# Recurrent mixer of the even layer without the products over constants that TensorE does while VectorE and ScalarE form weights

## What is computed

```python
def step(carry, inp):
    C, n, m = carry
    qc, kc, vc, ic, fc = inp
    b = jnp.cumsum(fc, axis=-1)
    log_d = jnp.where(tril, b[..., :, None] - b[..., None, :] + ic[..., None, :], -jnp.inf)
    log_inter = m[..., None] + b
    m_t = jnp.maximum(log_inter, jnp.max(log_d, axis=-1))
    w_intra = jnp.exp(log_d - m_t[..., None]) * jnp.einsum('bhtd,bhsd->bhts', qc, kc)
    ...
    num = (w_inter[..., None] * jnp.einsum('bhed,bhtd->bhte', C, qc)
           + jnp.einsum('bhts,bhse->bhte', w_intra, vc))
    ...
    C = decay[..., None, None] * C + jnp.einsum('bhs,bhse,bhsd->bhed', w_s, vc, kc)
```

## Time and profile before

| what | us |
|---|---|
| median of 3 runs | 3340.39 |
| the profiled execution's own time | 3338.58 |
| its span in the trace | 3336.8 |
| TensorE matmuls busy in the span | 3025.6 (91%) |
| mLSTM steps 2 to 5 (about 1997 to 2086 us of the span) | 89 |

### The profile page before, as it was taken

How to read it: one execution, slowest core, us unless ns; L and a number is a source line. 1 busy time by engine, 2 the same in 40 slices (tenths; PEclk the granted TensorE clock), 3 DMA queues, 4 the chain that set the end, 5 groups by cost and what they waited for, 6 DMA issues and landing times.

```text
span 3336.8 us, 41503 instructions
## 1 busy us (share of the span) xinstructions
PE 3025.6 (91%) x18502; PEld 2036.5 (61%) x18502; DVE 1112.0 (33%) x1572; ACT 877.3 (26%) x1320; POOL 0.2 (0%) x4
## 2 busy tenths in 40 slices
PE   6997899999997899999899988889999976999998
PEld 3775778888765777888677667554433353443443
DVE  3446632242536543223343347420000136000002
ACT  3443232232544233223433531311000032010001
POOL 0000000000000000000000000000000000000000
PEclk9998999999998899999899999889999997999999
DMA  7224323223233222222552041379999932999996
GB/s 267 78 99 152 103 76 98 92 95 95 79 116 148 68 89 89 92 92 95 177 163 74 13 192 62 106 294 409 409 408 409 401 133 101 364 409 409 408 409 268
DMA packets 247442, 637.27 MB, mean 191 GB/s; under 512 B 12896, under 2 KB 110176, under 8 KB 247136
## 3 DMA queue, kind: packets, MB, share of 16 engines
q1 hardware_dynamic: 244128, 627.22, 50.6%
q10 hardware_dynamic: 3136, 7.40, 0.6%
HBM read 632.48 MB, written 2.10 MB: 190 GB/s over the span
## 4 chain that ended last, share of the span: by engine, by line
PE 72%; DVE 8%; DMA 6%; ACT 5%; PEld 4%; issue 3%; PEldq 1%; SPq 1%; ACTq 0%; DVEq 0%
PE ps L612 69%; PEld ps L612 4%; DMA ring<-in_w_exp_gate 3%; PE ps L626 3%; ACT h L1580 1%; PEldq L1083 1%; DMA proj<-in_w_exp_gate 1%; ACT mix_halves L1583 1%; DMA ring<-in_w_exp_up 1%; DMA ring<-in_ada_w 1%; SPq L600 1%; ACT proj L1997 0%; DMA ring<-in_w_mod 0%; DVE work L2288 0%; DVE work L2881 0%
## 5 line engine op out<-in xcount | busy, mean ns | idle before, releaser
L612 PE MATMUL ps<-mix_halves,work_halves 128*128 128x512 f32 (+1 forms) x1544 | 622.1, 403 | 44.4 <-DVE h_halves L2139 34.4
L612 PE MATMUL ps<-h_halves,work_halves 128*128 128x512 f32 (+1 forms) x1544 | 608.9, 394 | 4.8 <-ACTq L1494 2.4
L612 PE MATMUL ps<-mix_halves,ring_halves 128*128 128x512 f32 x1448 | 568.3, 392 | 0.0
L2139 DVE TENSOR_TENSOR ring_halves<-ring,work_halves 128x2048 fp32r<-128x2048 f32 (+2 forms) x125 | 252.6, 2021 | 550.4 <-ACT work_halves L1503 453.9
L612 PE MATMUL ps<-ring,work 128*64 128x512 f32 x1680 | 389.1, 594 | 20.9 <-DMA ring<-in_w_exp_gate 18.2
L612 PEld LDWEIGHTS ps<-mix_halves,work_halves 128*128 128x128 f32 (+1 forms) x1544 | 290.8, 188 | 130.9 <-issue 48.8
L612 PEld LDWEIGHTS ps<-h_halves,work_halves 128*128 128x128 f32 (+1 forms) x1544 | 291.7, 189 | 72.6 <-issue 6.4
L612 PEld LDWEIGHTS ps<-mix_halves,ring_halves 128*128 128x128 f32 x1448 | 272.6, 188 | 60.8
L612 PEld LDWEIGHTS ps<-ring,work 128*64 128x64 f32 x1680 | 128.0, 137 | 254.6 <-issue 254.3
L2539 DVE SCALAR_TENSOR_TENSOR x<-ps,small,x 128x512 f32<-128x512 f32 x112 | 82.3, 750 | 598.5 <-PE ps L612 597.0
L1503 ACT ACTIVATE work_halves<-ring 128x2048 fp32r<-128x2048 f32 x102 | 188.2, 1845 | 337.2 <-PE ps L612 336.1
(11 more groups left out here) (377 smaller groups left out, 3318.1 us busy)
## 6 DMA issues: line engine op xcount, KB each, us to landing
ring<-in_w_exp_gate SPq DMA_DIRECT2D x114, 1024.0 KB, 11.3
ring<-in_w_exp_down SPq DMA_DIRECT2D x100, 1024.0 KB, 13.0
ring<-in_w_exp_up SPq DMA_DIRECT2D x96, 1024.0 KB, 15.2
ring<-in_ada_w SPq DMA_DIRECT2D x48, 1024.0 KB, 7.1
ring<-in_w_mod SPq DMA_DIRECT2D x48, 1024.0 KB, 7.5
proj<-in_w_exp_up SPq DMA_DIRECT2D x28, 1024.0 KB, 12.8
proj<-in_w_exp_down SPq DMA_DIRECT2D x28, 1024.0 KB, 15.9
ring<-in_w_in SPq DMA_DIRECT2D x22, 1024.0 KB, 5.3
```

The source lines that it names most:

```text
L612: i = pe.matmul(o, lhsT, rhs, start=start, stop=stop, **kw)
L2139: to("lo", tt(rounded(v), v, rounded(hi), ALU.subtract))
```

## The change

The helper `keep_busy` and its one call are taken out. In each of the steps 2 to 5 TensorE goes from the products of item 2 straight to the wait for `m_w`. Nothing else differs, except that lines behind the edit have numbers lower by 5 or 6.

```diff
             def mlstm():
 
-                def keep_busy(bank, times):
-
-                    for _ in range(times):
-                        mm(ps[:, bank, :], ident, consts[:, 0:T], True, True)
-
                 def vector(i, bank):
...
                         if step == 2:
                             mod_turn(4, 5)
                             pe.wait_ge(*due("mod_ready"))
-                        keep_busy(4, 6)
                         pe.wait_ge(*due("m_w"))
```

## The result

The changed kernel takes 3350.43 us (median of 7 runs, 3346.29 to 3355.72) against 3337.19 us (7 runs, 3329.89 to 3344.84) for the kernel before (the 3340.39 us ahead of the prediction is the median of the first three of these seven). The ratio is 1.0038, with a 95% interval of 1.0023 to 1.0054: slower by 0.38%, about 13 us. The forecast was 3352 us, with a range of 3343.5 to 3358.5; it was built on the profiled execution of before, 3338.58 us, and the profiled one of the changed kernel took 3351.80.

A forecast was written before the change was run, and what follows sets the result against it. VectorE and ScalarE bound each step's first part, TensorE the second. With the clock lost, 3 x 4.3 + 2.25 - 1.6 = 13.6 us on top of 3338.58 us gives 3352 us, range 3343.5 to 3358.5.

The forecast's parts named there:

- the first part of the prediction: In steps 2 to 5 VectorE and ScalarE set the first part, TensorE the second, some 8 us, where the price falls.
- The gain: Step 2: transposes start right behind line 2746 and end at 2010.42 instead of 2012.04, 1.6 us; steps 3 to 5 nothing.
- The cost: Second parts of steps 2 to 5 begin at 1.2 GHz: 4.3 us each in steps 2 to 4, 2.25 in step 5.
- transposes: Start of each step's second part: 8 transposes take 1.84 us at the low clock against 1.09, 0.75 us more.
- one-column products at the low clock: Behind the transposes: paced by their weight loads, 3.39 us against 1.86, 1.5 us more; lower bound nothing.
- values: The m_num products in each step's second part: 3.52 us at the low clock against 2.03, 1.5 us more.
- update, until the clock returns: Behind the values in steps 2 to 4: 1.1 us runs slowly, clock back 4.6 us after the values start; costs 0.55 us.
- step 5, both ends of the path: No update, values already slow: both ends move by what transposes and one-column products lose, 2.25 us.
- starts of steps 3, 4, 5: From the spreading to VectorE's pick-up: no difference, with bounds of 1.7 us less or 1.1 us more.
- The early return: Rival, steps 2 to 5: clock returns some 4.1 us after the first transpose; 6.0 us more, 3344.6 us; chance 0.16.
- That the clock outlasts the gap: Rival: clock stays high over gaps of 6.4 and 6.6 us; only the 1.6 us gain remains, 3337.0 us; chance 0.07.
- that it doesn't return before a step's end: Rival: update and last one-column products slow too, 6.9 us a step; 22.4 us more in all, 3361 us; chance 0.07.

The follow-up runs named there:

- the step 2 run: The kernel before with the six products over constants left out in step 2 alone, kept in steps 3 to 5: 3339.46 us, ratio 1.0013.
- the run with three and seven products: The kernel before with three products over constants in step 2 and seven in steps 3 to 5, instead of six: 3337.73 us, ratio 0.9995.

## Why the prediction was right

**The bound and the place.** All of the difference is in steps 2 to 5, and within them in the part that TensorE sets, as the first part of the prediction had it. VectorE's chain ahead of m_w keeps its length: from the start of line 2714 to the end of line 2740 it is 10.1 us in step 3 after (2025.36 to 2035.45), and 10.1 us from line 2720 to the end of line 2746 before.

**The gain.** Predicted 1.6 us in step 2. The first transpose stands 12.2 us into the stage (2009.14) instead of 13.8 (2011.01 in the timeline before), 1.6 us earlier. Three products in step 2 show the same with the clock held.

**The cost.** The table holds the terms of the sum against what they measured in steps 2, 3 and 4, as differences from one group's start to the next.

| term | predicted, us | measured, us |
|---|---|---|
| transposes | 0.75 | 0.8 to 0.9 |
| one-column products at the low clock | 1.5 | 1.6 |
| values | 1.5 | 1.5 to 1.7 |
| update, until the clock returns | 0.55 | 0, 0.2 and 0.5 |
| step 5, both ends of the path | 2.25 | 2.4 |
| starts of steps 3, 4, 5 | 0 | -0.9, -0.7, +1.3 |

The one-column products, for which no row stood at 1.2 GHz, took 3.41 us in every step: the upper end, and so the choice that they are paced by their weight loads, was right. With 64 columns they took 3.51 us, hardly more, which bears it out. The return of the clock came 3.1 to 4.6 us behind the start of the values, mostly sooner than the 4.6 us assumed, so the update's term was the one that was too large, by some 0.3 us a step. The values were priced a little too low: the 3.52 us that the prediction took as wholly slow ended at 2086.23, and the clock was back at 2085.8; wholly slow they took 3.73 to 3.76 us. By steps the stage grew 2.3, 3.4, 3.9 and 3.7 us, in all 13.2 us; the prediction's sum was 13.6.

Some of this closeness is luck. The starts of steps 3 to 5 add up to only -0.3 us because they cancel: step 5's alone cost 1.3 us, more than the 1.05 us that the prediction had for a slow start. In the second trace of the changed kernel they add up to -1.5 us, and its stage was 101.0 us. The second parts are where the sum was right: from the first transpose to VectorE's start on the last product they grew by 3.9, 4.3 and 4.6 us in steps 2 to 4, against the 4.3 of the forecast.

The slow stretches of the second parts are 8.1, 9.0 and 9.6 us in steps 2 to 4, together 26.7 us, and cost 12.8 us. (The 8.6 us of step 5 can't be added, since its values ran slowly before already.) The rule of the Trainium skill ("TensorE: Matmul & The Clock Gate", on the clock gate's oscillation) that a throttled stretch costs half of its length nearly holds for them: half is 13.3 us. In the prediction it gave 15.7 us, more than the 13.2 measured and than the 13.6 from rows, above all because it was applied to 9.8 us in each step. In what it says of iterations that begin at half rate, the trace agrees with it in all four steps.

**The rivals.** The early return, counted from the first transpose, did not happen: the clock returned 7.9 to 9.9 us after the first transpose in all four steps of both traces of the changed kernel. The reason that the prediction gave for this, that one-column products in between don't count, is not shown: with 64 columns the return came no sooner. What else delays it stays open; eight transposes and their copies are not the long row of transposes of the earlier trace rows. That the clock outlasts the gap is refuted by all four windows, and that it doesn't return before a step's end too.

The rule of the Trainium skill in the same page's part on transposes, that they don't count as work for the clock, is contradicted here: in the run with 48 transposes for the six products the clock was 1.00 at every second part that followed, and the stage took 89.1 us, as with products.

**The cause.** That the clock carries the loss is shown from three sides: the windows, the step 2 run, in which the same instructions run slowly in one step and fast in the next, and the pair of fillers, where transposes keep the time of before and almost empty products, which fill 3.6 of the 5.3 us, do not. What it is in the work that holds the clock, and what sets the moment at which it comes back, stays open.

## What to carry to other kernels

Work whose result nobody reads can be worth its place, when it fills a wait of TensorE ahead of a stretch in which TensorE sets the time: here some 21 us of such products kept 13 us off the path. Before such a group is taken out, look at two things in the trace: whether it ends before the wait's releaser (then removing it can't gain), and how long TensorE works in one piece behind the wait (here 8.1 to 9.6 us of it ran at the low clock). Here products of 512 columns and transposes did it and one-column products did not, and half of the group, placed at the start of the wait, lost most of the effect.

## What was not expected

- Transposes hold the clock as well as products do: 48 of them, 5.40 us, and the window behind reads 1.00 for 7.8 us.
- Sixteen products of one column in the same wait did not hold it; and where the clock fell among them they took 5.07 us instead of 3.6.
- The stage of the kernel before was 89.2 us in both traces, with the clock low in different places. In every variant that held the transposes at full clock in all four steps the clock still fell two or three times over the stage, more often than not at the start of a step. What it cost depended on where it fell: 1.05 us at the spreading products of step 3, next to nothing at the values of step 5, some 1.6 us a step at the values of steps 3 and 4 in the run with three and seven products.
